# Two-layer hybrid encoder step: attention from rounded halves, values stationary, probabilities normalised on Pool

## The reference

```python
xn = rmsnorm(x, norm_mix[l])
q, k, v, qi, ki, wi, u, gv = project(xn, w_in[l], pos)      # partial rotary on q, k, qi, ki
# dsa_attend: an indexer score picks topk keys for each query
rel    = relu(einsum('bthd,bsd->bths', qi, ki))
score  = einsum('bths,bth->bts', rel, wi) * scale           # chunk-causal
logits = einsum('btkgd,btskd->btkgs', qg, k_sel) * HEAD_DIM ** -0.5
p      = softmax(logits)
o      = einsum('btkgs,btskd->btkgd', p, v_sel)
gvn    = rmsnorm(gelu(gv), gate_norm[l])
bmix   = gelu(u) * spatial(gvn, w_spatial[l], b_spatial[l])
x = x + concat([o, bmix]) @ w_out[l]
x = x + relu(rmsnorm(x, norm_ffn[l]) @ w_ff1[l])**2 @ w_ff2[l]
```

## Time and profile before

| | us |
|---|---|
| median of 3 runs | 1511.53 (1510.69 to 1512.97) |
| span of the profiled execution, first to last instruction | 1508.3 |
| PE busy in it | 1483.1 (98%) |
| DVE busy | 664.4 (44%) |
| ACT busy | 521.8 (35%) |
| Pool busy | 185.1 (12%) |
| chain that ended last, on PE | 97% |
| of it L1334 (output projection and feed-forward) | 61% |
| of it L1108 (projections) | 15% |
| of it L1219, L1255, L1235, L1270, L1286 (attention stage) | 16% |

### The profile page before, as it was taken

One profiled execution on the slowest core, in us unless ns is written; L12 is line 12 of the kernel. 1 busy time (PEld: TensorE's weight loads), 2 busy tenths in 40 slices (PEclk: granted clock), 3 DMA queues, 4 the chain that ended last, 5 costly groups with the idle time before them and its releaser, 6 DMA issues.

```text
span 1508.3 us, 22280 instructions
## 1 busy us (share of the span) xinstructions
PE 1483.1 (98%) x9329; PEld 1323.6 (88%) x9329; DVE 664.4 (44%) x1172; ACT 521.8 (35%) x956; POOL 185.1 (12%) x215
## 2 busy tenths in 40 slices
PE   6999999999999999999999999999999999999997
PEld 5766766899999999999976677669999999999997
DVE  5257632245444444444623683213454444344453
ACT  5365542233213223133335553323332231321322
POOL 4246200020000000000214540000100000000011
PEclk8999755799999999999999995559999999999998
DMA  6211200033232222222321120001322222222221
GB/s 180 70 57 43 74 5 0 0 85 85 85 84 78 82 80 85 84 84 83 104 82 45 40 78 25 5 1 42 85 75 82 83 84 84 85 85 85 82 59 63
DMA packets 169252, 102.37 MB, mean 68 GB/s; under 512 B 6920, under 2 KB 159424, under 8 KB 169152
## 3 DMA queue, kind: packets, MB, share of 16 engines
q1 hardware_dynamic: 169152, 100.94, 23.0%
HBM read 96.98 MB, written 3.95 MB: 67 GB/s over the span
## 4 chain that ended last, share of the span: by engine, by line
PE 97%; DVE 1%; DMA 1%; ACT 1%; issue 0%; SPq 0%; DVEq 0%; ACTq 0%
PE bank L1334 61%; PE bank L1108 15%; PE bank L1219 6%; PE bank L1255 4%; PE bank L1235 3%; PE bank L1126 2%; PE bank L1270 2%; PE bank L1286 1%; PE bank L1140 1%; DMA late<-in_x_prompt 1%; PE bank L1200 1%; PE bank L1353 0%; PE bank L1069 0%; PE bank L1085 0%; ACT L677 0%
## 5 line engine op out<-in xcount | busy, mean ns | idle before, releaser
L521 ACT ACTIVATE ring_hi<-ring_raw 128x1024 fp32r<-128x1024 f32 x176 | 184.8, 1050 | 305.4 <-PE bank L1334 248.6
L1334 PE MATMUL bank<-vh,ring_hi 128*128 128x288 f32 x1280 | 275.4, 296 | 0.0
L1334 PE MATMUL bank<-vl,ring_hi 128*128 128x288 f32 x1280 | 275.2, 296 | 0.0
L1334 PE MATMUL bank<-vh,ring_lo 128*128 128x288 f32 x1280 | 275.2, 296 | 0.0
L766 DVE TENSOR_TENSOR ring_lo<-ring_raw,ring_hi 128x1024 fp32r<-128x1024 f32 x164 | 213.6, 1302 | 132.5 <-ACT ring_hi L521 125.5
L1334 PE MATMUL bank<-xh,ring_hi 128*128 128x288 f32 x1024 | 220.8, 297 | 0.0
L1334 PE MATMUL bank<-xl,ring_hi 128*128 128x288 f32 x1024 | 220.2, 296 | 0.0
L1334 PE MATMUL bank<-xh,ring_lo 128*128 128x288 f32 x1024 | 220.2, 296 | 0.0
L1334 PEld LDWEIGHTS bank<-vh,ring_hi 128*128 128x128 f32 x1280 | 205.2, 189 | 0.0
L1334 PEld LDWEIGHTS bank<-vh,ring_lo 128*128 128x128 f32 x1280 | 205.2, 188 | 0.0
L1334 PEld LDWEIGHTS bank<-vl,ring_hi 128*128 128x128 f32 x1280 | 205.2, 189 | 0.0
(11 more groups left out here) (161 smaller groups left out, 1608.9 us busy)
## 6 DMA issues: line engine op xcount, KB each, us to landing
ring_raw<-in_w_ff SPq DMA_DIRECT2D x128, 512.0 KB, 4.1
ring_raw<-in_w_in SPq DMA_DIRECT2D x32, 512.0 KB, 3.7
ring_raw<-in_w_out SPq DMA_DIRECT2D x16, 512.0 KB, 4.2
late<-in_x_prompt SPq DMA_DIRECT2D x4, 512.0 KB, 5.7
out_y_prompt<-late SPq DMA_DIRECT2D x4, 512.0 KB, 2.9
w_sp<-in_w_spatial SPq DMA_DIRECT2D x2, 512.0 KB, 4.2
gate_bc<-in_gate_norm SPq DMA_DIRECT2D x2, 256.0 KB, 4.9
out_k_prompt<-z SPq DMA_DIRECT2D x2, 256.0 KB, 4.3
```

The costliest lines, as they stand in the source:

```text
L521: s.activation(ring_hi[:, n % NSLOT, :], ring_raw[:, n % NRAW, :], ACT.Copy).then_inc(hi_ready, 1)
L1334: last = mm(bank[2 * (u % 4) + half][:, 0:HALF], w[:, k, :], a[:, k, HALVES[half]], start=k == order[0] and w is wh and a is ah, stop=k == ...
```

## The change

It touches the attention stage and what prepares it.

- Scores: q and k are split into halves (`q_hi`, `q_lo`, `k_hi`, `k_lo`, for the sample tile `ks_hi`, `ks_lo`), and `scores_of` adds three one-pass products, three items ahead and in three banks.
- q's transposes leave the projections: `q_transpose` of each tile is in the first five steps of attention, with `q_high` on ACT and `q_low` on DVE, all through bank 7.
- Heads are taken in groups of four that share a key/value head (10 groups). The exponential is in place, in one of eight buffers `pl`. After a group's four, DVE inverts the sums, and Pool multiplies the four probability rows by them, in place (40 multiplications for a layer).
- Then one step for each block of 128 keys of a group (24 steps for a layer): PE transposes the block of the four heads into one bank, ACT rounds the 512 columns (`p_high`), DVE subtracts (`p_low`), and PE multiplies with the values stationary (128 columns, both key/value heads) and the four heads' 512 columns moving, three products of halves (`weighted`). Its result is already transposed: `out_high` and `out_low` split it into `vh` and `vl`, 64 partitions for each group. `o_copy` and the transposes of its result are gone.
- The rows of `w_out` for the attention half are loaded in another order to fit this layout: three DMAs in place of one for each of the 8 units.
- The values are split as well (`values_high`, `values_low`), beside the projections; the keys' transposes are split in place of copied.
- Which step runs when is written out in `SLOT`: step s of group g is transposed in slot 4(g+1)+1+s and multiplied one slot later; slot i also does the scores of item i+3. `spatial` comes in the fifth slot of a tile and its transposes in the eighth.

```diff
+    NPL, AHEAD = 8, 3
+    NGR = NI // GQA
+    BLOCKS = [-(-KEYS[t] // P) for t in TILE_ORDER]
+    STEPS = [(g, s) for g in range(NGR) for s in range(BLOCKS[g // NKV])]
+    SLOT = {}
+    for g, s in STEPS:
+        SLOT.setdefault(GQA * (g + 1) + 1 + s, []).append((g, s))
+    LAST_SLOT = max(SLOT) + 2
+    MIX_AT, MT_AT = 4, 7
...
-        NTR = 13
+        NTR = 8
...
                 for j in range(KT):
-                    load(A["w_out"][l, :, j * P:(j + 1) * P].rearrange("(k p) n -> p k n", p=P), KT)
+                    raw = ring_raw[:, n[0] % NRAW, :].rearrange("p (k n) -> p k n", k=KT)
+                    for e in range(NKV):
+                        sp.dma_start(raw[HD * e:HD * e + HD, 0:GQA, :],
+                                     A["w_out"][l, DA // NKV * e:DA // NKV * (e + 1), j * P:(j + 1) * P]
+                                     .rearrange("(b d) n -> d b n", d=HD)).then_inc(wo_ready[n[0] % NRAW], 16)
+                    load(A["w_out"][l, DA:D, j * P:(j + 1) * P].rearrange("(k p) n -> p k n", p=P), KT, KT // 2)
...
+                for gr in range(NGR):
+                    a, t = gr // NKV, TILE_ORDER[gr // NKV]
+                    pool.wait_ge(rinv_ready, NGR * l + gr + 1)
+                    for i in range(GQA * gr, GQA * (gr + 1)):
+                        p = pl[0:ROWS[t], i % NPL, 0:KEYS[t]]
+                        g.tensor_scalar(p, p, rinv[0:ROWS[t], i:i + 1], None, ALU.mult).then_inc(p_ready, 1)
+                    if gr % NKV == 0:
+                        gated(a)
...
+                def p_high(g, k):
+                    act.wait_ge(pT_done, NS * l + k + 1)
+                    if k >= 2:
+                        act.wait_ge(o_step, NS * l + k - 1)
+                    s.activation(p_hi[0:n, k % 2, 0:GQA * ROWS[t]], bank[3 + k % 2][0:n, 0:GQA * ROWS[t]],
+                                 ACT.Copy).then_inc(p_hi_ready, 1)
...
+                act.wait_ge(idx_acc, NX * (l + 1))
+                q_high(0)
                 exp(0)
+                for i in range(LAST_SLOT):
+                    if i + 1 < NT:
+                        q_high(i + 1)
                     if i + 1 < NI:
                         exp(i + 1)
+                    for g, b in SLOT.get(i, ()):
+                        p_high(g, STEP_OF[g, b])
+                    for g, b in SLOT.get(i - 1, ()):
+                        if b == BLOCKS[g // NKV] - 1:
+                            out_high(g)
...
+                q_low(0)
+                mask_item(0)
+                mask_item(1)
+                for i in range(LAST_SLOT):
+                    if i + 1 < NT:
+                        q_low(i + 1)
+                    if i + 2 < NI:
+                        mask_item(i + 2)
+                    if i % GQA == GQA - 1 and i < NI:
+                        inverse_sums(i // GQA)
+                    for g, b in SLOT.get(i, ()):
+                        p_low(g, STEP_OF[g, b])
+                    for g, b in SLOT.get(i - 1, ()):
+                        if b == BLOCKS[g // NKV] - 1:
+                            out_low(g)
+                    if i < NI:
+                        if i % NH == 1 and i // NH + 1 < NT:
+                            gv_norm(TILE_ORDER[i // NH + 1])
+                        if i % NH == MIX_AT:
+                            mix_copy(i // NH)
+                        if i % NH == MT_AT:
+                            mt_low(i // NH)
...
+                    for a, k in ((q_hi, kh), (q_hi, kl), (q_lo, kh)):
+                        last = mm(bank[i % AHEAD][0:ROWS[t], 0:KEYS[t]], a[b:b + HD, hh % GQA, cols(t)], k[b:b + HD, 0:KEYS[t]],
+                                  start=a is q_hi and k is kh, stop=a is q_lo)
+                    last.then_inc(qk_done, 1)
...
+                def weighted(g, k):
+                    pe.wait_ge(p_lo_ready, NS * l + k + 1)
...
+                    for w, p in ((v_hi, p_hi), (v_lo, p_hi), (v_hi, p_lo)):
+                        last = mm(bank[5 + g % 2][:, 0:GQA * ROWS[t]], w[0:n, block, :], p[0:n, k % 2, 0:GQA * ROWS[t]],
+                                  start=b == 0 and w is v_hi and p is p_hi, stop=b == BLOCKS[a] - 1 and p is p_lo)
+                    last.then_inc(o_step, 1)
...
+                q_transpose(0)
+                for i in range(AHEAD):
+                    scores_of(i)
+                for i in range(LAST_SLOT):
+                    if i + 1 < NT:
+                        q_transpose(i + 1)
+                    if i + AHEAD < NI:
+                        scores_of(i + AHEAD)
+                    for g, b in SLOT.get(i, ()):
+                        p_transpose(g, STEP_OF[g, b])
+                    for g, b in SLOT.get(i - 1, ()):
+                        weighted(g, STEP_OF[g, b])
+                    if i < NI:
+                        if i % NH == MIX_AT:
+                            spatial(i // NH)
+                        if i % NH == MT_AT:
+                            mt_group(i // NH)
```

More of the change, by code:

```diff
@@ L35, in hybrid_encoder_program @@
     NH = DA // HD
+    GQA = NH // NKV
     NIH = 8
@@ L618, in tr_high, with values_high @@
                     s.activation(dst, bank[7][:, 0:width], ACT.Copy).then_inc(tr_hi, 1)
[L620 to L627, removed]
+                def values_high():
+                    act.wait_ge(small_in, 16 * 5 * (l + 1))
+                    if l:
+                        act.wait_ge(o_step, NS * l)
+                    s.activation(v_hi[:, 0:NPT, :], z[:, 0:NPT, Z_V:Z_V + DKV], ACT.Copy).then_inc(v_hi_ready, 1)
+                    s.activation(v_hi[0:DEC, SMP, :], z[0:DEC, SMP, Z_V:Z_V + DKV], ACT.Copy).then_inc(v_hi_ready, 1)
+                    s.activation(v_hi[:, NT, :], cache_v[:, :], ACT.Copy).then_inc(v_hi_ready, 1)
                 for n in range(S_OUT):
@@ L673, in exp @@
                     act.wait_ge(masked, NI * l + i + 1)
[L674 to L678, removed]
+                    p = pl[0:ROWS[t], i % NPL, 0:KEYS[t]]
+                    s.activation(p, p, ACT.Exp, scale=-1.0, bias=nmax[0:ROWS[t], i:i + 1],
                                  accum_out=rsum[0:ROWS[t], i:i + 1]).then_inc(exp_done, 1)
[L681 to L694, removed]
@@ L825, in tr_copy @@
                         return
[L826 to L831, removed]
+                    k = 4 * (n - 6)
+                    v.tensor_copy(w_spT[:, k:k + 4, :], bank[7][:, :].rearrange("p (g n) -> p g n", g=4)).then_inc(tr_evac, 1)
                     if n == 7:
@@ L922, in mt_low @@
[L922 to L929 removed]
+                    dve.wait_ge(q_hi_ready, NT * l + a + 1)
@@ L1202, in _, with q_transpose @@
                         last.then_inc(small_done, 1)
+                def q_transpose(a):
+                    t = TILE_ORDER[a]
+                    if a == 0:
+                        pe.wait_ge(q_roped, l + 1)
+                        pe.wait_ge(tr_evac, NTR * (l + 1))
+                    else:
+                        pe.wait_ge(q_lo_ready, NT * l + a)
+                    for b in range(4):
+                        last = tp(bank[7][:, b * ROWS[t]:(b + 1) * ROWS[t]], q[0:ROWS[t], t, b * P:(b + 1) * P],
+                                  ident[0:ROWS[t], 0:ROWS[t]])
+                    last.then_inc(qT_done, 1)
@@ L1239, in weighted @@
-                def weighted(i):
-                    t, hh = ITEMS[i]
-                    a = i // NH
-                    pe.wait_ge(pT_evac, NI * l + i + 1)
-                    if hh == 0 and a >= 2:
-                        pe.wait_ge(o_ready, NT * l + a - 1)
-                    nb = -(-KEYS[t] // P)
-                    g0 = Z_V + HD * (hh // 4)
-                    for s in range(nb):
-                        n = min(P, KEYS[t] - s * P)
-                        if t == SMP:
-                            vals = cache_v[:, HD * (hh // 4):HD * (hh // 4) + HD] if s == 0 else z[0:DEC, SMP, g0:g0 + HD]
-                        else:
-                            vals = z[:, s, g0:g0 + HD]
-                        last = mm(bank[4 + a % 2][0:ROWS[t], hh * HD:(hh + 1) * HD],
-                                  pT[0:n, i % 2, s * ROWS[t]:(s + 1) * ROWS[t]], vals, start=s == 0, stop=s == nb - 1)
-                    last.then_inc(o_item, 1)
+                    if hh == 0:
+                        pe.wait_ge(q_lo_ready, NT * l + i // NH + 1)
@@ L1285, in mt_group @@
                     for k in range(4):
-                        last = tp(bank[7 - part][:, k * ROWS[t]:(k + 1) * ROWS[t]], src[:, k * P:(k + 1) * P],
+                        last = tp(bank[7][:, k * ROWS[t]:(k + 1) * ROWS[t]], ug[0:ROWS[t], t, k * P:(k + 1) * P],
                                   ident[0:ROWS[t], 0:ROWS[t]])
                     last.then_inc(mt_done, 1)
-                scores_of(0)
-                scores_of(1)
-                spatial(0)
-                for i in range(NI):
-                    if i % NH == 4 and i > NH:
-                        spatial(i // NH)
-                    if i + 2 < NI:
```

(7 more changed lines are left out.)

258 lines of the change are left out of this document (142 added, 116 removed).

## The result

The changed kernel takes 1489.67 us (median of 4 runs, 1487.16 to 1491.58) against 1512.25 us: a ratio of 0.9849, 95% interval 0.9825 to 0.9872. That is faster by 1.5%, as to the sign, but four times less than the forecast 1423 us and outside its range of 1385 to 1480. It is within 3 us of what rival 2 (the clock stays low) gave.

What follows compares the result with a forecast made beforehand. PE was taken as the bound, slowed by low clock in attention: two stages from 253.9 to 170 us (83.9 less) and 4.4 from the projections, 88.3 less, a span of 1420.0 and median of 1423 us; range 1385 to 1480.

Steps and rivals of the forecast that it cites:

- rival 2: Attention stages: PE's repeated stops keep the clock low, 120 us a layer, 1493 us in all; chance 0.10.
- What bounds the kernel: Whole kernel: PE, busy 98% of 1508.3 us; attention's 124.2 and 129.7 us run at clocks of 0.57 and 0.54.
- The clock: New attention stage: about three quarters of PE's time is one-pass products, so full clock for nearly all of it.
- the high end of the range: Attention: Pool's dear multiplications plus part of the stage at low clock, 10 us a layer more: 1480 us.
- Pool's price: Group normalisation: a 512-column multiplication by a per-partition scalar taken near a copy's 0.61 us; 5 us a layer uncovered.
- rival 1: Attention groups: Pool is the bound at 3.3 ns an element, 24 instead of 5 us a layer uncovered, 1461 us; chance 0.11.
- The waits: New attention stage: PE's new waits at start, groups' first steps, Pool, end and DVE's order sum to 29 us.
- the product's wait: First step of each group: PE waits from transpose to product for `p_high` and `p_low`, ten times 0.9, 9 us.
- The 85 us: Length of each new attention stage: 55.7 us of PE work at full clock plus 29 us of waits.
- The work of PE: New attention stage at full clock: 42.8 us for items, 8.5 `spatial`, 2.2 gating and 2.2 q's transposes, sum 55.7 us.
- The projections: q's transposes and copies leave them: 2.2 us a layer less; splitting k and v costs nothing or 1 to 2 us.
- The other engines, the ring and the `w_out` loads: Attention: DVE about 52 us, ACT 48, Pool 24 to 39, all below 85; the `w_out` loads cost nothing.

Runs made afterwards that it cites:

- r5: Kernel before, its float32 scores reading all 128 partitions of q and k in place of 64 (logits of two heads added; times only): 1402.41 us, ratio 0.9271.
- r1: Changed kernel, its three score products reading all 128 partitions in place of 64 (logits of two heads added; times only): 1470.05 us.
- r3: Changed kernel, scores reading all 128 partitions and Pool multiplying only the first column of each probability row (times only): 1428.45 us.
- r8: Kernel before, whole computation, transposed keys kept per key/value head with zeros in the other's 64 partitions, scores reading 128: 1401.61 us, ratio 0.9265.
- r6: Changed kernel, whole computation, split keys padded with zeros so scores read 128 partitions, normalisation on VectorE in place of Pool: 1441.61 us, ratio 0.9525.
- r4: Changed kernel, whole computation, probabilities multiplied by the inverse sums on VectorE in place of Pool: 1482.23 us.
- r2: Changed kernel, Pool multiplying only the first column of each probability row by the inverse sum (times only): 1477.18 us.
- r11: r6 with each step's product two slots behind its transposes and q's transposes alternating between banks 7 and 6: 1417.29 us, ratio 0.9377.
- r7: Changed kernel, whole computation, keys padded with zeros so scores read 128 partitions, normalisation left on Pool: 1474.89 us, ratio 0.974.

## Why the prediction was wrong, step by step

- **What bounds the kernel**: right. The low clock was the cost of the stages, whose 124.2 and 129.7 us are the 253.9 that the sum starts from: with the clock at 1.00 and 0.98, r5 has 70.6 us in each. That it came with "float32 scores and weighted values" pointed at the right instructions, the scores, by the wrong property: r5 changes only the number of partitions that they read, and the clock is at 1.00 and 0.98.
- **The clock** is the step that failed. It said that every long stretch of one-pass products is at 1.00, and so is the one with indexer products over 32 partitions. Both rows are true, and the conclusion does not follow: in the projections (60 to 130 us) the products over 32 partitions are about a quarter of PE's matmul time and lie between long ones over 128, while the scores of the changed kernel over 64 are a third to a half of PE's time. With the same one-pass products, over 64 partitions: 0.59 and 0.67; over 128: 0.77 and 0.82 (r1), 0.88 with Pool's stops gone (r3). Why the projections keep 1.00 was not tested.
- **Transposes** don't explain the low clock either: r5 and r8 have as many of them as before and are at 0.98 to 1.00 in both stages. In the changed kernel the last steps, rich in transposes, are at 1.00 (277 to 286.8 us), and the stretch of scores and products before them (260 to 277 us) is at 0.50. The 10 us a layer of low clock in the high end of the range were the author's estimate, and no run shows them: in layer 0 of the changed kernel 172 to 180 us are at 0.50, as is the stretch up to 277 us, and the whole stage is at 0.59.
- **Rival 2** had the time, 1493, and not the mechanism: a stage at half clock costs the same whatever holds the clock down, so the agreement is luck as to the cause. Its premise was stops; the row from 249 to 260 us has none and stands at 0.50, and in r1 PE stops for longer (26 and 28 us against 16 and 17) and the clock is higher (0.77 and 0.82 against 0.59 and 0.67). Stops explain at most a rest: r3 and r6 still have 0.88 and 0.87, with 17 and 19 us of idle time, and r8 has 1.00 with 2.7. In r6 the clock falls at 172 us (0.98 in the two us before, 0.50 in the two after), behind PE's wait of 2.5 us at the stage's start, and from 203 us on it is at 1.00.
- **Pool's price** is the second term that was mis-sized: 0.61 us taken, 1.56 measured at 512 columns, and 0.60 for the 0.29 at 128. Beyond a start of 0.19 us (an estimate from the 203 ns for five columns) that is 2.7 us for each thousand columns at 512, within the bound of 3.3 kept for rival 1. The factor of 2.1 in the prediction compares two operations on Pool; Pool against VectorE, on the same multiplication, is the 3.2 of r4. At low clock it costs 12.5 us (r2), less than rival 1's 38, since a slow PE covers it; at the high clock, r1 against r3, 42.
- **The waits** were put too high as a sum, 24 us without Pool's 5, against 17.5 us of idle time in r3. For the product's wait 9 us were put down, and 10.4 are in r3. For the start 8 were put down, and PE's waits for `q_low` are 4.8 in r3. The 85 us come near r3's 88 because the half clock left in r3 (0.88 on the mean, some 10 us by an estimate from it) makes up for this.
- **The work of PE**: the distances of products at full clock were right at 512 columns (0.23 us in r6's scores and weighted values); at 128 they are 0.11 in r6 and not 0.08, and 0.11 us apart start two weight loads of 128 columns as well (230.69 and 230.80 us in r6). What was not worked out is the same table for the old kernel at full clock. It would have shown 0.91 + 0.44 + 0.84 = 2.19 us for an item of tile 3 against 1.84 in the new one: 0.35 us, some 10 us a stage over all tiles, to be set against 29 us of new waits. All of the forecast gain was the clock. The restructuring by itself was a loss: of the 22 us a layer between r6 and r8 (1441.6 and 1401.6 us in all) some 10 are its own, by the estimate above. With the longer chain and the second bank (r11) 1417.3 us are left, still 15.7 more than r8; how much of that is the clock of 0.91 was not separated.
- **The projections**: 2.2 us a layer were to be won, about 1 was. The last unbroken run of projections in layer 0 begins at 130.69 us and not at 129.32. Of these 1.4 us, 0.6 are there at 57 us already, where nothing had changed for PE (the run of 60 products that begins at 19.5 us took 16.3 us in place of 15.6), and 0.8 came between 60 and 130 us, beside the added splits on ACT and DVE; which of them did it was not tried.
- **The other engines, the ring and the `w_out` loads**: DVE is busy for 43% and 46% of the two stages, and no wait on the ring or the loads showed, as forecast. In r6, at higher clock and with the normalisation on it, DVE is busy for 68% of the stage.

## What to carry to other kernels

Look at the granted clock before counting passes: where it is at 0.50 with PE never idle there may be up to a factor of two to win, by an estimate from the clock alone (here 124 and 130 us, at 0.57 and 0.54, became 71 at 1.00 and 0.99), and the cheapest way to it may be to let the products read all 128 partitions, here with zeros in half of them, for 7.3% and a dozen lines. Work out both versions at both clocks; a restructuring that pays at the clock you hope for may pay only because of that clock. And when an engine gets faster, the engines that it hid come out: measure a new instruction form on the slow engine (here Pool with a per-partition scalar) before a chain is put behind it.

## What the runs showed of the hardware

- With scores over 64 partitions, about half of PE's time, TensorE stayed at 0.50 through 11 us without a gap (the changed kernel, 249 to 260 us); with scores over 128 partitions, half of them zeros, it rose (0.87, 0.81 and 1.00 in layer 0 of r6, r7 and r8). Why the chip does so no run shows, and the share of such products at which it turns was not measured. Nor was it tried whether it matters that the scores change between the lower and the upper 64 partitions every four heads.
- Products over 64 partitions do not hold the clock down always. With the same program, layer 0 has 0.59 and layer 1 0.67, since in layer 1 it rose at 973 us in the middle of tile 3's scores (0.50 from 972 to 973 us, 0.94 in the two us after) and stayed up for some 10 us. And one run of the kernel before took 1470.19 us at a mean clock of 0.949. Over 128 partitions every run of r5 and r8 has 0.989 or more.
- A float32 multiplication by a per-partition scalar in SBUF, 128x512: 1.56 us on Pool (the changed kernel), 0.48 on DVE (r4). Pool's product of two tensors is cheaper (1.27) than its product by a scalar.
